# A two-block fp32 network: the split weights moved 32 bytes further off the activations' raster

## What is computed

```
proj = rmsnorm(x) @ gla_w_in            # 2048 x 6160
x = x + (gla(proj) * silu(r)) @ gla_w_out
x = x + relu(rmsnorm(x) @ mlp_w_up)**2 @ mlp_w_down      # 2048 x 8192, 8192 x 2048
...
proj = rmsnorm(x) @ w_in_2              # 2048 x 14336
x = x + (g_a * y_a + g_b * y_b + g_c * y_c) @ w_out_2
x = x + relu(rmsnorm(x) @ w_mlp_up_2)**2 @ w_mlp_down_2
return rmsnorm(x)
```

## Time and profile before

| what | value |
|---|---|
| device time, median of 3 runs | 2740.0 us |
| lowest and highest of them | 2737.16 and 2740.21 us |
| the profiled execution's own time | 2741.1 us |
| its span, from the first instruction to the last | 2739.3 us |
| PE matmul busy | 2717.0 us, 99% |
| PE weight load busy | 2386.3 us, 87% |
| VectorE (DVE) busy | 1785.3 us, 65% |
| ScalarE (ACT) busy | 1347.6 us, 49% |
| HBM | 184 GB/s over the span |

### The profile page before, as it was taken

One profiled execution on the slowest core, in us unless ns is written; L12 is line 12 of the kernel. 1 busy time (PEld: TensorE's weight loads), 2 busy tenths in 40 slices (PEclk: granted clock), 3 DMA queues, 4 the chain that ended last, 5 costly groups with the idle time before them and its releaser, 6 DMA issues.

```text
span 2739.3 us, 43483 instructions
## 1 busy us (share of the span) xinstructions
PE 2717.0 (99%) x15611; PEld 2386.3 (87%) x15611; DVE 1785.3 (65%) x2056; ACT 1347.6 (49%) x1629; POOL 73.6 (3%) x60
## 2 busy tenths in 40 slices
PE   8999999999999999999999999999999999999998
PEld 7888888888888888888888888888888888888887
DVE  5666766656566567766887666666666565665664
ACT  5546554444444445544675554554554444444443
POOL 1000010000000002200000000000100000000001
PEclk9999999999999999999999999999999999999999
DMA  6784655565566565665456555655556665665653
GB/s 203 167 207 130 193 189 186 188 188 184 186 187 191 187 189 183 192 209 171 155 177 189 188 184 184 191 191 192 184 184 188 188 186 190 186 188 189 186 184 131
DMA packets 507186, 504.45 MB, mean 184 GB/s; under 512 B 17843, under 2 KB 505544, under 8 KB 507096
## 3 DMA queue, kind: packets, MB, share of 16 engines
q1 hardware_dynamic: 505820, 501.60, 58.6%
q10 hardware_dynamic: 1276, 1.63, 1.4%
HBM read 499.50 MB, written 3.67 MB: 184 GB/s over the span
## 4 chain that ended last, share of the span: by engine, by line
PE 97%; DVE 2%; ACT 0%; issue 0%; DMA 0%; POOL 0%; SPq 0%; DVEq 0%; ACTq 0%; POOLq 0%
PE acc L500 59%; PE acc L502 30%; PE acc L495 3%; PE acc L497 2%; DVE wsp L1070 0%; DVE lat L1367 0%; DMA xtok<-in_x 0%; PE misc L604 0%; PE misc L619 0%; PE misc L724 0%; DVE z L1080 0%; ACT wsp L778 0%; PE misc L586 0%; PE misc L573 0%; PE misc L516 0%
## 5 line engine op out<-in xcount | busy, mean ns | idle before, releaser
L1070 DVE TENSOR_TENSOR wsp<-raw,wsp 128x1024 fp32r<-128x1024 f32 x944 | 1167.2, 1244 | 624.1 <-ACT wsp L778 593.4
L500 PE MATMUL acc<-xs,wsp 128*128 128x512 f32 x4224 | 1486.9, 396 | 1.5 <-DVE wsp L1070 1.5
L778 ACT ACTIVATE wsp<-raw 128x1024 fp32r<-128x1024 f32 x944 | 993.3, 1056 | 736.3 <-PE acc L502 654.0
L502 PE MATMUL acc<-xs,wsp 128*128 128x256 f32 x4224 | 1187.4, 281 | 0.0
L500 PEld LDWEIGHTS acc<-xs,wsp 128*128 128x128 f32 x4224 | 794.4, 188 | 181.2 <-DVE wsp L1070 2.3
L500 PE MATMUL acc<-hs,wsp 128*128 128x512 f32 x2560 | 897.9, 395 | 0.0
L502 PEld LDWEIGHTS acc<-xs,wsp 128*128 128x128 f32 x4224 | 802.2, 190 | 0.4
L502 PE MATMUL acc<-hs,wsp 128*128 128x256 f32 x2560 | 719.4, 281 | 0.0
L500 PEld LDWEIGHTS acc<-hs,wsp 128*128 128x128 f32 x2560 | 480.9, 188 | 107.8
L502 PEld LDWEIGHTS acc<-hs,wsp 128*128 128x128 f32 x2560 | 486.0, 190 | 0.0
L787 ACT ACTIVATE corr<-acc 128x512 f32<-128x512 f32 x247 | 147.6, 598 | 402.3 <-PE acc L502 393.3
(11 more groups left out here) (219 smaller groups left out, 997.4 us busy)
## 6 DMA issues: line engine op xcount, KB each, us to landing
raw<-in_w_in SPq DMA_DIRECT2D x224, 512.0 KB, 4.4
raw<-in_mlp_w_up SPq DMA_DIRECT2D x128, 512.0 KB, 3.9
raw<-in_mlp_w_down SPq DMA_DIRECT2D x128, 512.0 KB, 4.3
raw<-in_w_mlp_up SPq DMA_DIRECT2D x128, 512.0 KB, 3.9
raw<-in_w_mlp_down SPq DMA_DIRECT2D x128, 512.0 KB, 4.3
raw<-in_gla_w_in SPq DMA_DIRECT2D x96, 512.0 KB, 4.5
raw<-in_gla_w_out SPq DMA_DIRECT2D x32, 512.0 KB, 4.2
raw<-in_w_out SPq DMA_DIRECT2D x32, 512.0 KB, 3.7
```

What stands on the lines that cost most here:

```text
L500: pe.matmul(acc[:, g, j], w_part(0, slot)[:, t, cols], x[:, k0 + k], start=start, stop=False, skip_group_check=True)
L502: ins = pe.matmul(acc[:, g, j, 1], w_part(1, slot)[:, t, cols], x[:, k0 + k, 0], start=False, stop=stop, skip_group_check=True)
L778: act.activation(w_part(0, slot), raw[:, slot], ACT.Copy).then_inc(hi_done, 1)
L1070: dve.tensor_tensor(w_part(1, slot), raw[:, slot], w_part(0, slot).bitcast(F32), ALU.subtract).then_inc(lo_done, 1)
```

## The change

One constant grows by 8 elements, which is 32 bytes. LOWS is counted from the high parts and stays, so both parts move: the high ones to 96 and the low ones to 288 bytes off the raster. The last element used is then 8312 of 8320. No instruction is added, removed or moved on any engine; the addresses of `wsp` in the instructions of lines 778, 1070, 495, 497, 500 and 502 are all that differs.

```
--- before.py
+++ after.py
@@ -127,7 +127,7 @@
 
     KB = 1024
     raw = at("raw", [P, SLOTS, UK, NB])
-    HIGHS, LOWS = 16, SLOTS * UK * NB + 48
+    HIGHS, LOWS = 24, SLOTS * UK * NB + 48
     wsp = at("wsp", [P, 2 * SLOTS * UK * NB + P], F32R)
 
     def w_part(k, slot):
```

## The result

The changed kernel takes 2720.1 us (median of 4 runs, 2719.3 to 2721.5) against 2740.1 for the kernel before, a ratio of 0.9929 with a 95% interval of 0.9912 to 0.9946: 0.7% faster. The profiled execution's span is 2718.8 us, 20.5 less than before. Forecast was no change, 2740, so the likeliest case was the wrong one; the time lies in the range, 3 us above what the rival "a better step" gives for 346.7 ns.

A forecast was written before the change was run, and what follows sets the result against it. The prediction took the distance between PE's matmuls to bound the kernel; 2741.1 us profiled, plus 0 for the change, minus 1.1 to the median of runs, gave 2740 us, range 2701 to 2768.

The forecast's parts named there:

- the likeliest case: Long stretches keep their pair time: no change, within some 3 us of 2740, own range 2735 to 2745; chance 0.40.
- a better step: Long stretches lock at 346.7 ns (2717 us) or 340.0 (2672 us), or a mixture (2702 us); chance 0.30.
- What bounds the kernel: Whole kernel: PE busy 99% of the span, nearly nothing but the distance between matmuls sets the time.
- The splits of ACT and DVE at zero: Lines 778 and 1070: 1056 and 1244 ns, a few per cent either way hidden behind PE in long stages: zero.
- nothing from the DVE-bound blocks: The 12 blocks xr, scc and scx: quicker pairs gain nothing; 1% in line 1070 is 0.6 us.
- I take zero steps: Lines 500 and 502: the 6784 pairs on the path keep their mean; each 3.33 ns step would be 22.6 us.
- The comparison with the gate projection: Gate projection, weights 64 and 256 bytes less off the raster: its pair is within a step of gk 3's.
- the pair comes in steps: Matmul pairs take 340.0, 346.7, 350.0 or 353.3 ns, in units of 3.33 ns, 8 columns or 32 bytes.
- both MLPs at 340.0: MLP 1 and MLP 2 begin luckily and lock at 340.0 ns: 38 us gained, 2702 us.
- a worse step: Lines 500 and 502 in every block: one 3.33 ns step a pair more, 2763 us; two, 2785; chance 0.30.
- one piece of 64 bytes more to a load: Weight loads at odd multiples of 32 bytes touch one more piece if reading goes by 64 bytes; 3.33 ns a pair.
- Its share for lines 495 and 497: Lines 495 and 497, where weights are the moving operand: at most 13 ns x 384 = 5 us.

The follow-up runs named there:

- the run at 64/272: Kernel before the change with the low parts alone moved by 16 bytes, to 272, high parts staying at 64: 2672.2 us, ratio 0.9752.
- the last run: PE alone, network left out: six pairs of offsets in changing order, stretches of 12, 16 and 32 pairs; at 64/16 both 340.0 and 346.7 ns a pair.
- two maps: PE alone, network left out: high and low offsets varied in steps of 32, then 16 bytes, two stretches of 12 pairs each; finer mean 349.2 ns.
- 192/272: Kernel before the change with the high parts moved to 192 and the low parts to 272 bytes off the raster: 2675.7 us, ratio 0.9765.

## Why the prediction failed

**What bounds the kernel**: right. Only the distance between matmuls counts, and 6784 pairs times its change gave the time: 10 ns were 68 us by the prediction and 67 in the run at 64/272.

**The splits of ACT and DVE at zero, and nothing from the DVE-bound blocks**: right, 1244 and 1055 ns, and 0.1 us for the 12 blocks.

**The step that failed** is "I take zero steps". Its reason was that gk 2, gk 3 and the rest differ at one offset, "so the offset alone doesn't decide the pair". This is true, and the last run shows it at its purest. But from "not alone" I went on to "nearest to no change", and that doesn't follow. The offset fixes which states there are (340.0, 350.0 and 353.3 at 64/256, but 343.3 and 352 to 353 at 96/288), and how a stretch begins, with what ran before it, picks one. None of the states seen at the new offset is the old 350.0: the term put at zero measured +2.0 ns a pair in MLP 1 and -6.7 in mix and MLP 2, -18.4 us in the long stretches. So the case that I held likeliest could come out only if gains and losses cancelled. The 32 bytes, which I noted as the unit of the steps and then set aside, should have weighed more; even 16 bytes give other states. The comparison with the gate projection, "within a step" at 64 and 256 bytes less, was of no use: a step is 22.6 us, four times the smallest change that can be told. And "the pair comes in steps" of 3.33 ns holds for the four values that I had, not for 352.0 or 351.1.

**The rival "a better step"**: near in size (2717 at 346.7, measured 2720), but by luck, since no stretch of 20 pairs or more with stationary weights ran at 346.7. A mixture is what happened, though not the one priced, both MLPs at 340.0: MLP 1 got worse, 352.0, and mix and MLP 2 better, 343.3. That it comes because "the two streams inside PE meet less often at the new offset" is not borne out: with PE alone over 64 beginnings the new offset is worse by 2.3 ns, and the mean of the kernel's own stretches, each counted once, is 349.2 against 349.6.

**The rival "a worse step"**: it holds in sign for MLP 1 and the go stage, +5 us, at 2.0 ns a pair and not 3.33. Its reason, one piece of 64 bytes more to a load, isn't shown. Its share for lines 495 and 497 came out right in sign and within its bound of 5 us: gv and v rose from 346.7 to 353.3, about 2.5 us in 384 pairs.

**What would show it**: the test at the end, "if different windows of one trace have different pairs, the offset is not what counts but where a stretch begins", was put as an either-or. It is both.

**Open.** Which readings of PE meet: a run that moves xs, and one that leaves the loads out, would tell. In the traces the load of weights takes 188 to 190 ns in all states, while the distance from line 500 to 502 goes from 226.7 ns (at 340.0) to 234.2 (in MLP 1 after) and that from 502 to 500 from 113.3 to 117.8. What carries the state from one stretch over an interruption to the next, and why 256 bytes is the period. What makes some executions differ: three of the ten runs of the kernel with the low parts alone at 288 took 2748 to 2751 us and seven 2737 to 2739. A stretch that begins otherwise could do that (MLP 2 at 351.1 in place of 346.7 would be an estimated 8 us), but no trace of the longer ones exists.

## What to carry to other kernels

Where the chain is one engine's own back-to-back work, read its pitch stage by stage from windows; if identical instructions have two pitches in one trace, the time is partly a draw, and a change of 0.7% may be a new draw and no improvement. Such a thing is measured with a kernel in which the engine runs alone through many offsets and many beginnings: here two maps cost 2.3 ms of device time each and found 67 us where single tries on the full kernel had found 20. Such a map names candidates and no more: 192/272 was at 340.0 in all its beginnings with PE alone and at 353.6 in two stretches of the kernel, 64/272 was at 346.7 in all 32 beginnings of one run and at 340.0 in the long stretches of the kernel. So run the candidates in the full kernel, read every stretch there, and do it again after each edit ahead of a long stretch.

## What was not expected of the hardware

- The pitch of a float32r pair (512 and 256 columns, each with its load of 128 columns) hangs on where the stationary operands stand, modulo 256 bytes, in steps of 16 bytes or finer, with the moving operand in one place: 340.0 to 355.7 ns with PE alone at the full granted clock.
- The values are few and stable: 340.0, 343.3, 346.7, 350.0, 353.3 and some between. Read closely, each is a pattern that repeats, mostly of one to five pairs, and those are a whole number of 6.67 ns long (700.0 ns in two pairs, 1760.0 in five). At one offset up to three are stable.
- The state outlives an interruption of the row by one small matmul, so that a stretch's pitch depends on what ran before it, up to 340.0 against 346.7 ns for the same addresses and the same beginning.
